# Two weight chunks in one transfer, in a kernel of two transformer blocks on one core

## The reference, cut to what matters

```python
# first block
xn = rms_norm(h, gain);  proj = xn @ w_in                 # 2048 x 6160
h = h + concat(forgetting_attention, dilated_attention) @ w_out   # 2048 x 2048
hn = rms_norm(h, gain)
q = hn @ w_query                                          # 2048 x 2048
vals, idx = top_k(q . sub_keys);  experts, gates = top_k of the sums, softmax
u = take(expert_down, experts); v = take(expert_up, experts)      # 16384 experts of 2048
h = h + (gates * gelu(u . hn)) @ v
# second block
proj = rmsnorm(x) @ w_in                                  # 2048 x 5136
x = x + concat(window attention, gated linear attention, stick-breaking attention) @ w_out
x = x + square(relu(rmsnorm(x) @ w1)) @ w2                # 2048 x 8192 and 8192 x 2048
out = rmsnorm(x)
```

## Time and profile before

| | |
|---|---|
| median of 3 runs | 3116.03 us (3115.39 to 3116.09) |
| the profiled execution | 3111.83 us |
| its span, from the first to the last instruction | 3110.0 us |
| PE busy | 3073.7 us (99%) |
| PEld, DVE, ACT, POOL busy | 84%, 57%, 47%, 21% |
| DMA on SP's queue | 156544 packets, 549.79 MB, 56.8% of 16 engines |
| all DMA | 627.60 MB, mean 202 GB/s |
| mean granted TensorE clock | 0.996 |

### The profile page before, as it was taken

How to read it: one execution, slowest core, us unless ns; L and a number is a source line. 1 busy time by engine, 2 the same in 40 slices (tenths; PEclk the granted TensorE clock), 3 DMA queues, 4 the chain that set the end, 5 groups by cost and what they waited for, 6 DMA issues and landing times. The chain is left out here.

```text
span 3110.0 us, 40502 instructions
## 1 busy us (share of the span) xinstructions
PE 3073.7 (99%) x14724; PEld 2609.2 (84%) x14724; DVE 1773.8 (57%) x2339; ACT 1464.2 (47%) x1822; POOL 638.3 (21%) x455
## 2 busy tenths in 40 slices
PE   8999999999999999999999999999999999999998
PEld 7999888888888888888888888899888888888886
DVE  5445554689864444565565556645776454545444
ACT  5444454554544444444444444554565444444453
POOL 3110000088888887000000000000000000000000
PEclk9999999999999999999999999999999999999999
DMA  6764467688888778777776775654446666666664
GB/s 217 244 203 135 136 202 253 194 217 217 216 218 221 214 219 249 272 238 239 238 230 212 226 250 182 190 181 147 127 140 186 187 191 189 189 190 187 191 186 148
DMA packets 215975, 627.60 MB, mean 202 GB/s; under 512 B 58139, under 2 KB 58789, under 8 KB 215472
## 3 DMA queue, kind: packets, MB, share of 16 engines
q1 hardware_dynamic: 156544, 549.79, 56.8%
q0 software_dynamic: 54464, 59.30, 7.7%
q10 hardware_dynamic: 4848, 16.94, 1.4%
HBM read 587.78 MB, written 38.14 MB: 201 GB/s over the span
## 5 line engine op out<-in xcount | busy, mean ns | idle before, releaser
L571 DVE TENSOR_TENSOR w_lo<-raw,w_hi 128x1024 fp32r<-128x1024 f32 (+2 forms) x1072 | 1280.0, 1196 | 1167.5 <-ACT w_hi L566 1164.7
L566 ACT ACTIVATE w_hi<-raw 128x1024 fp32r<-128x1024 f32 (+2 forms) x1072 | 1106.6, 1034 | 1342.0 <-PE ps L1612 1034.0
L1610 PE MATMUL ps<-w_hi,a_hi 128*128 128x512 f32 x1536 | 601.4, 392 | 0.0
L1612 PE MATMUL ps<-w_hi,a_lo 128*128 128x512 f32 x1536 | 598.1, 389 | 0.0
L1611 PE MATMUL ps<-w_lo,a_hi 128*128 128x512 f32 x1536 | 597.8, 389 | 0.0
L1610 PE MATMUL ps<-w_hi,x_hi 128*128 128x512 f32 x1504 | 587.3, 390 | 0.0
L1612 PE MATMUL ps<-w_hi,x_lo 128*128 128x512 f32 x1504 | 585.4, 389 | 0.0
L1611 PE MATMUL ps<-w_lo,x_hi 128*128 128x512 f32 x1504 | 585.2, 389 | 0.0
L468 POOL DMA_INDIRECT gates<-srch x256 | 518.4, 2025 | 151.3 <-issue 77.5
L1761 PE MATMUL ps<-w_hi,x_hi 128*128 128x440 f32 (+2 forms) x1184 | 450.4, 380 | 2.4 <-DVE x_lo L1046 2.4
L1763 PE MATMUL ps<-w_hi,x_lo 128*128 128x440 f32 (+2 forms) x1184 | 438.1, 370 | 0.0
(11 more groups left out here) (336 smaller groups left out, 1714.3 us busy)
## 6 DMA issues: line engine op xcount, KB each, us to landing
raw<-in_peer_down SPq DMA_DIRECT2D x256, 512.0 KB
raw<-in_peer_up SPq DMA_DIRECT2D x256, 512.0 KB
raw<-in_w_mlp_in SPq DMA_DIRECT2D x128, 512.0 KB
raw<-in_w_mlp_out SPq DMA_DIRECT2D x128, 512.0 KB
raw<-in_w_in SPq DMA_DIRECT2D x112, 440.0 KB
raw<-in_w_in SPq DMA_DIRECT2D x96, 428.0 KB
raw<-in_w_out SPq DMA_DIRECT2D x64, 512.0 KB
gates<-zero POOLq DMA_DIRECT2D x32, 512.0 KB, 4.8
```

Source lines behind the costliest of these rows:

```text
L566: act.activation(w_hi[:, c % RING, 0:2 * n], raw[:, c % RING, 0:2 * n], ACT.Copy).then_inc(hi_made, 1)
L571: nc.vector.tensor_tensor(w_lo[:, c % RING, 0:2 * n], raw[:, c % RING, 0:2 * n], w_hi[:, c % RING, 0:2 * n].bitcast(F32), ALU.subtract).th ...
L1610: mm(o, xh, wh, start=(k == 0), stop=False)
L1612: last = mm(o, xl, wh, start=False, stop=(k == KT - 1))
```

## The change

`load` is called for every chunk as before but does nothing for odd ones. For an even chunk it waits for what the odd one waited for, and issues one transfer for both: from two neighbouring chunks in memory (or two that lie a constant step apart, in the output projections) into two neighbouring buffers of `raw`, up to 1 MB. There is one semaphore for each pair of buffers, and ACT's split of either chunk waits for it. The number of buffers, the splits, the matmuls and the order of the chunks stay.

```diff
-        raw_loaded = [sem(f"raw_loaded{i}") for i in range(RING)]
+        raw_loaded = [sem(f"raw_loaded{i}") for i in range(RING // 2)]
...
-            def load(B, c, src):
-                q = SUB * B + c
+            def load(B, c, rows):
+
+                if c % 2:
+                    return
+                q = SUB * B + c + 1
                 if not static(q) or q >= RING:
                     sp.wait_ge(lo_made, q - RING + 1)
-                n = src.shape[1] * src.shape[2]
-                sp.dma_start(raw[:, c % RING, 0:n], src.rearrange("p k n -> p (k n)")).then_inc(raw_loaded[c % RING], 16)
+                n = rows.shape[2] * rows.shape[3]
+                sp.dma_start(raw[:, c % RING:c % RING + 2, 0:n],
+                             rows.rearrange("c p k n -> p c (k n)")).then_inc(raw_loaded[c % RING // 2], 16)
+
+            def two(w, order, s):
+
+                (_, b, c), (_, b1, c1) = order[s:s + 2]
+                i, j = SUB * b + c, SUB * b1 + c1
+                return w.rearrange("b c p k n -> (b c) p k n")[i:j + 1:j - i]
...
-                            load(b0 + 8 * r + i, c, w[4 * (first_round + r) + i % 4, c])
+                            load(b0 + 8 * r + i, c, w[4 * (first_round + r) + i % 4, c // 2 * 2:c // 2 * 2 + 2])
...
-                load(s // SUB, s % SUB, weights[name][b, c])
+                if s % 2 == 0:
+                    load(s // SUB, s % SUB, two(weights[name], SEQ, s))
...
-                        w = a["peer_up"][4 * nu + i, c] if up else a["peer_down"][4 * nd + i, c]
+                        at = slice(c // 2 * 2, c // 2 * 2 + 2)
+                        w = a["peer_up"][4 * nu + i, at] if up else a["peer_down"][4 * nd + i, at]
...
-                load(b0 + s // SUB, s % SUB, weights[name][b, c])
+                if s % 2 == 0:
+                    load(b0 + s // SUB, s % SUB, two(weights[name], SEQ2, s))
...
-            act.wait_ge(raw_loaded[c % RING], 16 * (2 * B + c // RING + 1))
+            act.wait_ge(raw_loaded[c % RING // 2], 16 * (2 * B + c // RING + 1))
```

## The result

| | before | after |
|---|---|---|
| median | 3115.31 us (3113.67 to 3116.09, 6 runs) | 3127.02 us (3125.87 to 3128.7, 6 runs) |
| profiled execution, its span | 3111.83 us, 3110.0 us | 3127.14 us, 3125.3 us |

The ratio is 1.0039, with a 95% interval of 1.0028 to 1.0051. The change makes the kernel 11.7 us slower. The forecast was 3116.3 us and the range ended at 3124.0, so both missed.

What follows compares the result with a forecast made beforehand. PE's matmuls were taken as the bound. Start +0.1 us, other places 0 and 0.2 us set aside made 3111.83 into 3112.1 us; the median's 4.2 us distance gave 3116.3 us, range 3114.0 to 3124.0.

Steps and rivals of the forecast that it cites:

- The loads are paced by the ring, the ring by PE: Whole kernel: weight loads wait for free raw buffers, and these for PE's matmuls; 177 us of saved SP issuing worth nothing.
- Landing, 5.0 us: Every pair: 1 MB lands 5.0 us after issue, with bounds of 4.2 and 8.3 us.
- The MLP, 0: Steady MLP stage: a pair may take 5.8 us before ACT notices, about 11.4 us before PE does; cost 0.
- The search, 0: Expert search, 600 to 870 us: ACT's even split 1.75 us late, but covered by DVE's own backlog; cost 0.
- the limit for DVE is 6.3 us: Expert search: a pair may take 6.3 us to land before DVE's second split of the even chunk is held.
- The turn at 1224 us, 0 to 2 us: Turn to the second expert phase, 1224 to 1252 us: late splits still covered; cost 0, at most 2 us.
- The start, +0.1 us: First transfer grows from 440 to 880 KB, taken as 1.2 us; PE's first matmul +0.1 us, bounds -0.5 to +1.2.
- A: Search, 600 to 870 us: pairs land too late; 3131 us at a 7.2 us landing, 3185 at 8.3; chance 12%.
- 3% for rows 512 KB apart: A partition's two rows lie 512 KB apart; by a skill rule this costs 3% of the data time.
- B: Two late bursts: the start costs its full 1.2 us and the turn at 1224 us 2 us; 3119 us, chance 15%.
- C: Larger transfers run ahead: at best 1 us of PE's 8.7 us wait at the start returns; 3115 us, chance 8%.
- D: The runtime splits each pair into two loads, all else as before; 3116 us, its chance counted inside the forecast.

Runs made afterwards that it cites:

- the run meant for it: The changed kernel with the five instructions of each top-16 search step replaced by two copies of a constant row, so the same experts are chosen: 3618.25 us, ratio 1.1646.

## Why the prediction was wrong, step by step

- **"The loads are paced by the ring, the ring by PE"**: right, and it is why 472 pairs cost nothing. SP's issues saved nothing, as foreseen; it waits more than before:

```profile
SPq L405 <- DVE w_lo L584: 2789.2, 532, 10.7
```

- **Landing, 5.0 us**: right. From issue to the end of the last packet it was 3.7 us in the middle for a single load of the search before, and 4.7 for a pair after (nine in ten under 5.4, the longest 6.8); in the MLP 3.4 and 4.5. By the Trainium skill ("DMA: Bandwidth & Descriptors", "Anatomy of one DMA"), whose fit is for transfers issued from GpSimd and not from SP as here, the second 512 KB is worth 1.2 us as an estimate; the traces show 1.0 to 1.1.
- **The MLP, 0**: right. ACT's splits there are released by PE, after as before:

```profile
2722.25 1.06 ACT L579 ACTIVATE w_hi<-raw 128x1024 fp32r<-128x1024 f32 x1 [1.66 <-PE ps L1625]
```

- **The search, 0**: wrong, and it is 10 us of the 11.7. The step that failed is "the limit for DVE is 6.3 us" and the price built on it, that PE pays only from a landing of 6.9 us. Three things were wrong in it. First, it was read from the even half of one pair, at 640 us, with the ring as it stood before the change: there PE had 2.6 us of cover, while the odd half of the same pair had 1.9 us, as little as any chunk of the search. Second, it took DVE's idle 29.2 us as a sum to give away. DVE's idle time isn't where it is needed. In the trace of before DVE stands idle for 1.66 us at 696 us because ACT's drain is in front of the split, and that very chunk has 3.8 us of cover where the one before it had 5.6. In the steps after it DVE starts its splits 2.84 us apart against PE's 2.72 us a chunk (later steps of a block take up to 3.5):

```profile
697.54 1.23 DVE L571 TENSOR_TENSOR w_lo<-raw,w_hi 128x1024 fp32r<-128x1024 f32 x1 [1.66 <-ACT w_hi L566]
...
700.38 1.23 DVE L571 TENSOR_TENSOR w_lo<-raw,w_hi 128x1024 fp32r<-128x1024 f32 x1
...
703.22 1.23 DVE L571 TENSOR_TENSOR w_lo<-raw,w_hi 128x1024 fp32r<-128x1024 f32 x1
```

  So through most of a block of search steps (14 chunks) DVE falls behind and eats cover, and it wins it back only in the last few. There the late issue bites: before, the cover is 5.0 to 5.6 us again at the end of every block; with the change it is 3.6 us at 700 us and never above 3.2 us from 703 us to the end of the search, since DVE then stands waiting for a split that waits for the landing (the 4.03 us before 701.54 above). The next block starts from that and uses it up. Third, the sum over one turn of the ring (landing, one first split, two second splits; 8.5 of 10.9 us) was done only for the MLP. In the search a step of some 1.6 us (2.84 - 1.23) lies between DVE's splits, and the landing has 0.4 us before ACT starts: 4.7 + 0.4 + 1.1 + 1.2 + 1.6 + 1.2 = 10.2 of 10.9 us. Nothing is left for the drain (1.3 + 1.3 us), which the prediction had only as "ACT's other instructions" and without a price, nor for a pair that lands in 6.8 us.
- **Where the edge is**, from the runs: from the issue of the load or pair to ACT's split of the even chunk, the medians over the search (chunks 184 to 309) are 3.9 us with two transfers waited for singly (loss 0.05 us), 4.4 with every load one later (2.4 us), 5.1 when both are waited for (8.4 us) and 5.2 with the change (10.1 us). So 1.2 to 1.3 us of the median separate free from the full price. The median alone doesn't give the loss, though: it is 5.2 us with pairs only in the search (7.2 us lost) and 5.3 with the drain moved (5.6 us lost).
- **The turn at 1224 us, 0 to 2 us**: 0.5 to 0.7 us is lost in the two traces of the change, at 1211 us, just ahead of it; nothing between 1224 and 1260. Three other runs with pairs there, the two with singles in the search and that with eight raw buffers, lose nothing.
- **The start, +0.1 us**: PE's first weight matmul came at 13.07 and not at 12.26, +0.8 us, since the first 880 KB landed at 8.82 and not at 6.95; the term of 1.2 us for 440 KB more was 1.9. It doesn't stay: see the run with singles at the start. So this miss is not in the total.
- **The rivals.** A named the right mechanism, place and sign, and its test held: DVE's idle time in the 270 us rose from 29 to 42 us and PE shows waits for w_lo. But it was priced as a line through one wrong point, so it had 12%, and by its sum a landing of 4.7 us was free. Its 3% for rows 512 KB apart doesn't bear on this kernel either: in the Trainium skill ("DMA: Bandwidth & Descriptors", "Latency and other measured facts") the row pitch is from one partition to the next, which here is 4 KB, and no cost of it shows in the landings above. B's two bursts leave 0.5 to 0.7 us, ahead of the turn, and nothing of the start. C and D are out: the queue shows 536 loads, most of 1024 KB.
- **The account**: 11.7 us between the medians; 10.0 in the search, 0.5 to 0.7 at 1211 us, and about 1 us that the spread of the runs (2.4 and 2.8 us) doesn't let me place.

Two things stay open. The loss of the pairs in the search was 7.2 us with single loads around it and 10 us with pairs; I did not look for what makes that difference, and each is one trace. And how the rest of the loss, some 5 to 6 us once the drain is moved, divides between DVE's search steps and late landings wasn't shown, since the run meant for it failed.

## What to carry to other kernels

When transfers are joined over a ring of buffers, do the sum of one turn of the ring (landing, notice, every reader in turn, with whatever stands between them in each engine's order) in the stretch where the readers are busiest, not where they are calm. An idle share is no reserve: ask whether the idle time comes before the moment that needs it. If the whole is waited for, the ring needs more places: with eight this kernel lost nothing; six, two more as the pair takes, was not tried. With four places issued together but waited for one by one it lost nothing either, with 0.24 us to spare. And since PE waits for no weight transfer, no form of the change made it faster.

## What the runs showed of the hardware

- **Issuing together makes the DMA engines' work shorter; joining does not.** Packets, MB and share of the span for the weight loads, from the pages of the kernel before and of the run with two transfers issued together:

```profile
q1 hardware_dynamic: 156544, 549.79, 56.8%
```

```profile
q1 hardware_dynamic: 156544, 549.79, 52.1%
```

  The same packets take 4.7 points less of 16 engines when two loads of 512 KB are issued back to back, and 52.2% as pairs of 1 MB. The other runs agree, the failed one aside: 51.2 to 52.4% in those with most loads in twos, joined or not, 56.9% with single loads issued one chunk later but still spaced, and 56.0% with pairs in the search alone. It is no gain in time here.
- **Indirect writes of the gates to the same few experts went with slow DMA.** With the same experts chosen for each token the DMA engines moved 105 GB/s at 96% busy, against 214 GB/s at 80%. The 128 additions of one transfer then go to 128 neighbouring words of the table, and those of all heads to the same ones. That this is the cause is the likeliest reading, as no transfer was added, but it wasn't isolated.
- **Two rows of a partition 512 KB apart cost nothing to see**: a pair took 1.0 to 1.1 us longer than a single load (medians, 4.7 against 3.7 us in the search and 4.5 against 3.4 in the MLP), less than the 1.3 us that 512 KB take at the 400 GB/s of the earlier trace rows.
